# One of three dense tiles' gates put into a cleared DRAM table by GpSimd's adding scatters, and 52 low halves made by VectorE

## The reference, cut to what matters

```python
q = (xt @ wq).reshape(t_len, 8, 2, 64)
sub = jnp.einsum('thpd,hpkd->thpk', q, subkeys)        # 128 keys a half
s_top, i_top = lax.top_k(sub, 16)
cand = s_top[:, :, 0, :, None] + s_top[:, :, 1, None, :]
sc, ci = lax.top_k(cand.reshape(t_len, 8, 256), 16)
i1 = take(i_top[:, :, 0], ci // 16); i2 = take(i_top[:, :, 1], ci % 16)
eid = (i1 * 128 + i2).reshape(t_len, 128)              # 128 picks of 16384 experts a token
gate = jax.nn.softmax(sc, axis=-1).reshape(t_len, 128)
h = gelu(jnp.einsum('cd,ced->ce', xc, u[ec]))
out = jnp.einsum('ce,ced->cd', gate * h, v[ec])
```

## Time and profile before

| | before |
|---|---|
| median of 3 runs | 1693.93 us (1693.28 to 1694.68) |
| span of the profiled execution | 1695.2 us |
| TensorE busy | 1674.3 us (99%) |
| VectorE busy | 1206.4 us (71%) |
| GpSimd busy | 810.8 us (48%) |
| ScalarE busy | 779.4 us (46%) |
| moved by DMA | 417.63 MB, 246 GB/s on the mean |

### The profile page before, as it was taken

How to read it: one execution, slowest core, us unless ns; L and a number is a source line. 1 busy time by engine, 2 the same in 40 slices (tenths; PEclk the granted TensorE clock), 3 DMA queues, 4 the chain that set the end, 5 groups by cost and what they waited for, 6 DMA issues and landing times.

```text
span 1695.2 us, 24483 instructions
## 1 busy us (share of the span) xinstructions
PE 1674.3 (99%) x9013; PEld 1481.6 (87%) x9013; DVE 1206.4 (71%) x2480; ACT 779.4 (46%) x1318; POOL 810.8 (48%) x491
## 2 busy tenths in 40 slices
PE   9999999999999999999999999999999999999997
PEld 7778777788899999999999999999888888888886
DVE  3586895511164885989888988434988888888886
ACT  4545545522324345773675477433333333333332
POOL 5332233444542667776776776774433323323312
...
DMA  5121121242421566997899799997999999999952
GB/s 205 63 75 50 63 75 63 100 139 98 143 94 44 184 215 211 373 381 252 287 386 359 226 332 371 370 369 293 405 389 355 367 387 347 383 382 347 389 194 87
DMA packets 126502, 417.63 MB, mean 246 GB/s; under 512 B 12976, under 2 KB 32432, under 8 KB 124848
## 3 DMA queue, kind: packets, MB, share of 16 engines
...
q0 software_dynamic: 36864, 134.23, 21.1%
q10 hardware_dynamic: 19200, 49.03, 7.4%
...
...
## 4 chain that ended last, share of the span: by engine, by line
PE 90%; DMA 3%; DVE 3%; POOL 2%; ACT 1%; issue 1%; SPq 0%; ACTq 0%; DVEq 0%
PE ps L1364 17%; PE ps L1365 17%; PE ps L1366 17%; PE ps L1626 10%; PE ps L1624 10%; PE ps L1623 10%; PE ps L1734 5%; PE ps L1476 1%; DMA raw<-u_units 1%; PE ps L1428 1%; POOL w_lo L500 1%; POOL w_lo L458 1%; PE ps L1459 1%; DMA raw<-w_units 1%; DMA u_got<-u_rows,eid 1%
## 5 line engine op out<-in xcount | busy, mean ns | idle before, releaser
L557 ACT ACTIVATE w_hi<-raw 128x1024 fp32r<-128x1024 f32 x330 | 348.9, 1058 | 395.0 <-PE ps L1626 294.4
L1364 PE MATMUL ps<-tok_hi,w_hi 128*128 128x384 f32 (+1 forms) x1472 | 525.9, 357 | 3.1 <-ACT gelu_t L748 1.7
L1365 PE MATMUL ps<-tok_lo,w_hi 128*128 128x384 f32 (+1 forms) x1472 | 516.9, 351 | 0.0
L1366 PE MATMUL ps<-tok_hi,w_lo 128*128 128x384 f32 (+1 forms) x1472 | 516.9, 351 | 0.0
L500 POOL TENSOR_TENSOR w_lo<-raw,w_hi 128x1024 fp32r<-128x1024 f32 x128 | 318.4, 2490 | 166.1 <-ACT w_hi L557 165.0
L458 POOL TENSOR_TENSOR w_lo<-raw,w_hi 128x1024 fp32r<-128x1024 f32 x76 | 181.7, 2395 | 318.0 <-ACT w_hi L557 317.8
L1364 PEld LDWEIGHTS ps<-tok_hi,w_hi 128*128 128x128 f32 x1472 | 276.5, 188 | 33.8 <-issue 12.0
L1623 PE MATMUL ps<-w_hi,gh_hi 128*128 128x512 f32 x760 | 295.7, 389 | 0.0
L1624 PE MATMUL ps<-w_lo,gh_hi 128*128 128x512 f32 x760 | 295.7, 389 | 0.0
L517 POOL DMA_INDIRECT v_got<-v_rows,eid x128 | 150.0, 1172 | 304.1 <-DVE own L1148 286.9
L1366 PEld LDWEIGHTS ps<-tok_hi,w_lo 128*128 128x128 f32 x1472 | 276.3, 188 | 18.1
...
## 6 DMA issues: line engine op xcount, KB each, us to landing
raw<-u_units SPq DMA_DIRECT2D x128, 512.0 KB
raw<-v_rows SPq DMA_DIRECT2D x128, 512.0 KB
raw<-w_units SPq DMA_DIRECT2D x78, 512.0 KB
...
```

The lines of the kernel that those rows point to most:

```text
L557: act.activation(hi_of(n), raw[:, n % RAW, :], ACT.Copy).then_inc(hi_done, 1)
L1364: pe.matmul(out_, l_hi, r_hi, start=start, stop=False)
L1365: pe.matmul(out_, l_hi, r_lo, start=False, stop=False)
L1366: return pe.matmul(out_, l_lo, r_hi, start=False, stop=stop)
```

## The change

The gates of tile 1 no longer go through TensorE. SP clears the first four of the twelve bodies of `gate_d` with 16 stores of zeros of 512 KB (`clear_gates`, issued among the loads of units 8 to 23; the zeros are written by GpSimd once, in `zero`). VectorE works out for each token and pick the address in the table (`put_at`) and leaves the gates in `g_put`. GpSimd then issues 128 indirect DMAs, one a pick (`put_gate`), which add 4 bytes for each of the 128 tokens at their places in the table. Two heads of a token can pick the same expert, while the 16 picks of one head are all different: so every sixteenth put first waits until all earlier ones have landed.

Only 64 quads are left. Their two stages now have 26 units each, and a unit has one or two quads (`quads_in`). The units are laid out anew: routing of tile 1 in units 16 to 29, of tile 2 in 30 to 43, mark stage 2 in 44 to 69, routing of tile 3 in 70 to 83, mark stage 3 in 84 to 109, tail from 110. Two lists of points (`PACE`) set how many dots and puts must be out by which unit. VectorE makes the low halves of two in three units of the mark stages and of all in the tail (`low_on_dve`, `unit_lo`): 17 + 17 + 18 = 52 of 128 by the program's table; GpSimd keeps 76.

```diff
 
 DT = S - P
 NB = DT // TOK
-N_QUAD = DT // 4
-FIRST_UNITS, ROUTE_UNITS, MARK_UNITS = 16, 14, 16
-TAIL = FIRST_UNITS + 3 * (ROUTE_UNITS + MARK_UNITS)
-ROUTE_DOTS, MARK_DOTS = (3, 6, 6), 30
+PUT_TOK = P
+PUT_BODIES = PUT_TOK // TOK
+N_QUAD = (DT - PUT_TOK) // 4
+FIRST_UNITS, ROUTE_UNITS, MARK_UNITS = 16, 14, 26
+MARK_AT = {2: FIRST_UNITS + 2 * ROUTE_UNITS, 3: FIRST_UNITS + 3 * ROUTE_UNITS + MARK_UNITS}
+ROUTE_AT = {1: FIRST_UNITS, 2: FIRST_UNITS + ROUTE_UNITS, 3: MARK_AT[2] + MARK_UNITS}
+TAIL = MARK_AT[3] + MARK_UNITS
+PACE = {"dots": ((FIRST_UNITS + 6, 0), (ROUTE_AT[2], 3), (MARK_AT[2], 7), (ROUTE_AT[3], 45), (MARK_AT[3], 50),
+                 (TAIL, 90), (P - 4, P)),
+        "puts": ((ROUTE_AT[2] + 1, 0), (MARK_AT[2], 13), (ROUTE_AT[3], 59), (MARK_AT[3], 72), (TAIL, 118),
+                 (TAIL + 5, P))}
 U_SLOTS, V_SLOTS = 5, 6
 FMA_START, FMA_END = 2, P - 12
 KEPT = 8
 GATE_GROUP, GELU_GROUP = 16, 4
 
 
-def routed_at(j):
-
-    return FIRST_UNITS + (j - 1) * (ROUTE_UNITS + MARK_UNITS)
-
-
-def dots_before(b):
-
-    return sum(ROUTE_DOTS[:b]) + MARK_DOTS * b
+def by_unit(kind, k):
+
+    points = PACE[kind]
+    for (k0, n0), (k1, n1) in zip(points, points[1:]):
+        if k < k1:
+            return n0 + max(0, n1 - n0) * max(0, k + 1 - k0) // (k1 - k0)
+    return points[-1][1]
 
 
 def dots_by(k):
 
-    if k < FIRST_UNITS:
-        return 0
-    b, at = divmod(k - FIRST_UNITS, ROUTE_UNITS + MARK_UNITS)
-    if k >= TAIL:
-        return min(P, dots_before(3) + (P - dots_before(3)) * (k - TAIL + 1) // (P - TAIL - 4))
-    if at < ROUTE_UNITS:
-        return dots_before(b) + ROUTE_DOTS[b] * max(0, at - 6) // (ROUTE_UNITS - 7)
-    return dots_before(b) + ROUTE_DOTS[b] + MARK_DOTS * (at - ROUTE_UNITS + 1) // MARK_UNITS
+    return by_unit("dots", k)
+
+
+def quads_in(k):
+
+    return range(32 * k // MARK_UNITS, 32 * (k + 1) // MARK_UNITS)
+
+
+def low_on_dve(k):
+
+    return MARK_AT[2] <= k < ROUTE_AT[3] and k % 3 > 0 or MARK_AT[3] <= k < TAIL and k % 3 > 0 or TAIL <= k < P
+
+
+LOW_DVE = [k for k in range(P) if low_on_dve(k)]
+LOW_POOL = [k for k in range(P) if not low_on_dve(k)]
 
 
 def right_by(q):
...
                 sp.dma_start(gelu_in[m % 2][:], gelu_d[:, first:first + GELU_GROUP, :])\
                     .then_inc(gelu_back[m % 2], 16)
 
+            def clear_gates(i):
+
+                body, line = i // 4, P // 4 * (i % 4)
+                if i == 0:
+                    sp.wait_ge(zero_set, 1)
+                sp.dma_start(gate_d[body, :, line:line + P // 4, :].rearrange("p j t -> p (j t)"), zero[:])\
+                    .then_inc(zeros_out, 16)
+
             for j in range(P):
                 load_unit(U_EXP + j, u_units[j])
+                if 8 <= j < 8 + 4 * PUT_BODIES:
+                    clear_gates(j - 8)
                 if j == P - 8:
                     sp.wait_ge(gate_read, N_QUAD)
                     for s in range(2):
-                        sp.wait_ge(stage_out[s], 16 * (NB // 2))
+                        sp.wait_ge(stage_out[s], 16 * (NB - PUT_BODIES) // 2)
+                    sp.wait_ge(put_out, 16 * P)
                     load_gates(0, 0)
                 if j == P - 4:
                     load_gates(0, 1)
...
                 if e >= U_SLOTS:
                     pool.wait_ge(dot_done, e - U_SLOTS + 1)
                 elif e == 3:
-                    pool.wait_ge(pick_set, 2)
+                    pool.wait_ge(put_set, 1)
                 pool.indirect_dma_start(
                     out=u_got[e % U_SLOTS][:], out_offset=None, in_=u_rows,
                     in_offset=bass.IndirectOffsetOnAxis(ap=eid[:, e:e + 1], axis=0)).then_inc(u_in[e % U_SLOTS], 16)
...
                     out=v_got[e % V_SLOTS][:], out_offset=None, in_=v_rows.rearrange("p a d -> (p a) d"),
                     in_offset=bass.IndirectOffsetOnAxis(ap=eid[:, e:e + 1], axis=0)).then_inc(v_in[e % V_SLOTS], 16)
 
-            got = [0]
+            def put_gate(e):
+
+                if e == 0:
+                    pool.wait_ge(zeros_out, 16 * 4 * PUT_BODIES)
+                    pool.wait_ge(put_set, 1)
+                elif e % EK == 0:
+                    pool.wait_ge(put_out, 16 * e)
+                pool.indirect_dma_start(
+                    out=gate_d.rearrange("b p j (t o) -> (b p j t) o", o=1),
+                    out_offset=bass.IndirectOffsetOnAxis(ap=put_at[:, e:e + 1], axis=0),
+                    in_=g_put[:, e:e + 1], in_offset=None, compute_op=ALU.add).then_inc(put_out, 16)
+
+            got, put = [0], [0]
+
+            def puts_to(n):
+                while put[0] < min(n, P):
+                    put_gate(put[0])
+                    put[0] += 1
 
             def rows_to(n):
                 while got[0] < min(n, P):
...
                     got[0] += 1
 
             for k in range(FIRST_UNITS):
+                if k == 4:
+                    pool.wait_ge(sub_full, 16)
+                    pool.memset(zero[:], 0.0).then_inc(zero_set, 1)
                 expert_lo(k)
             pool.wait_ge(eid_set, 1)
             rows_to(3)
             for k in range(FIRST_UNITS, P):
-                expert_lo(k)
+                if not low_on_dve(k):
+                    expert_lo(k)
                 rows_to(dots_by(k - 1) + U_SLOTS if k >= FIRST_UNITS + ROUTE_UNITS else 3)
+                puts_to(by_unit("puts", k))
             rows_to(P)
             for s in range(2):
-                pool.wait_ge(stage_out[s], 16 * (NB // 2))
+                pool.wait_ge(stage_out[s], 16 * (NB - PUT_BODIES) // 2)
             for e in range(P):
                 get_v(e)
             pool.wait_ge(ln2_in, 32)
...
                 dve.tensor_tensor(w_lo[:, n % RAW, :], raw[:, n % RAW, :], w_hi[:, n % RAW, :].bitcast(F32),
                                   ALU.subtract).then_inc(lo_dve, 1)
 
+            def unit_lo(k):
+
+                n = U_EXP + k + LO_AHEAD
+                dve.wait_ge(hi_done, n + 1)
+                dve.tensor_tensor(w_lo[:, n % RAW, :], raw[:, n % RAW, :], w_hi[:, n % RAW, :].bitcast(F32),
+                                  ALU.subtract).then_inc(lo_dve, 1)
+
             def dot(e):
 
                 dve.wait_ge(u_in[e % U_SLOTS], 16 * (e // U_SLOTS + 1))
...
                 if b == 0:
                     dve.scalar_tensor_tensor(eid[:], pick[:, 0, :], float(NK), pick[:, 1, :], ALU.mult, ALU.add)\
                         .then_inc(eid_set, 1)
+                if b == 1:
+                    dve.wait_ge(lane_set, 1)
+                    settled(dve.tensor_scalar(part, lane, 5, None, ALU.logical_shift_right))
+                    dve.scalar_tensor_tensor(first_at, part, float(P * P * TOK - TOK), lane, ALU.mult, ALU.add)
+                    settled(dve.scalar_tensor_tensor(c_row[:], pick[:, 0, :], float(NK), pick[:, 1, :], ALU.mult, ALU.add))
+                    dve.tensor_scalar(put_at[:], c_row[:], float(TOK), first_at, ALU.mult, ALU.add)
                 dve.wait_ge(gexp_done, b + 1)
                 g = pick[:, 2, :].rearrange("p (h k) -> p h k", h=EH)
                 settled(dve.tensor_reduce(g_sum[:, 0, :], g, mybir.AxisListType.X, ALU.add))
                 settled(dve.reciprocal(g_sum[:, 1, :], g_sum[:, 0, :]))
-                to = g_own if b == 0 else pick[:, 2, :]
-                dve.tensor_tensor(to[:].rearrange("p (h k) -> p h k", h=EH), g,
+                to = (g_own[:], g_put[:], pick[:, 2, :], pick[:, 2, :])[b]
+                dve.tensor_tensor(to.rearrange("p (h k) -> p h k", h=EH), g,
                                   g_sum[:, 1, :].unsqueeze(2).to_broadcast([P, EH, EK]), ALU.mult)\
-                    .then_inc(pick_set, 1)
+                    .then_inc(put_set if b == 1 else pick_set, 1)
 
             def spread_picks(b):
 
-                dve.wait_ge(pickT_full, b)
-                if b > 1:
-                    dve.wait_ge(gate_full, 32 * (b - 1))
+                dve.wait_ge(pickT_full, b - 1)
+                if b == 3:
+                    dve.wait_ge(gate_full, 32)
                 dve.tensor_copy(g_T[:], ps[:, 5, 2 * P:3 * P]).then_inc(pickT_set, 1)
 
             def mark(q):
...
             route(0)
             dve.wait_ge(own_x, 1)
             for b in range(1, NT):
-                parts = iter([dots_before(b - 1) + ROUTE_DOTS[b - 1] * i // 3 for i in (1, 2, 3)])
+                parts = iter([dots_by(ROUTE_AT[b] + ROUTE_UNITS * i // 3 - 1) for i in (1, 2, 3)])
                 route(b, lambda: dots_to(next(parts)))
+                if b == 1:
+                    continue
                 spread_picks(b)
                 for k in range(MARK_UNITS):
-                    for quad in (2 * k, 2 * k + 1):
-                        mark(32 * (b - 1) + quad)
-                    dots_to(dots_by(routed_at(b) + ROUTE_UNITS + k))
+                    if low_on_dve(MARK_AT[b] + k):
+                        unit_lo(MARK_AT[b] + k)
+                    for quad in quads_in(k):
+                        mark(32 * (b - 2) + quad)
```

(12 more changed lines are left out.)

62 lines of the change are left out of this document (36 added, 26 removed).

## The result

| | before | changed |
|---|---|---|
| median of 4 runs each, same chip | 1693.72 us (1693.28 to 1694.68) | 1798.92 us (1796.56 to 1801.37) |
| ratio to before | | 1.0617, 95% interval 1.0602 to 1.0633 |
| span of the profiled execution | 1695.2 us | 1796.8 us |

The changed kernel is 105 us slower. I had forecast 1673.0, in a range of 1662 to 1708, and gave 0.24 to slower.

A forecast was written before the change was run, and what follows sets the result against it. TensorE was taken as the bound, the DMA engines as second limit. 1695.2 - 28.6 (quads) - 0.3 (transposes) + 4 (GpSimd's waits) + 4 (tail) = 1674.3 us profiled, 1673.0 median; range 1662 to 1708.

The forecast's parts named there:

- The bound and TensorE's loss: TensorE is the bound, busy 1674.3 of 1695.2 us; dropping 32 of 96 quads and three transposes saves 28.9 us.
- The clearing: Units 8 to 23: 16 stores of 512 KB, costed at nothing; 23 us of the DMA engines if uncovered.
- VectorE: Loses 49.0 us, gains 52 low halves at 1.24, 64.5 us; fits mark stages, and the tail if no dot waits.
- The put's price: GpSimd, units 44 to 110: put spacing 1.25 us, bounds 1.25 to 1.47; 313.5 us of work against TensorE's 331.8.
- rival C: GpSimd becomes the bound between units 44 and 110: 1705 us, or 1728 with spacing 1.47; chance 0.23.
- a put longer than 1.5 us: Sign on GpSimd that would by itself overturn the forecast, as would a landing over 8 us.
- What a put costs that is priced right: GpSimd, unit 44 to the tail: waits 10 us over the free 18, mostly hidden; 4 us left on the path.
- The waits for landings: On GpSimd every sixteenth put waits until earlier ones have landed: seven waits of 4 us, 28 us.
- The clock: TensorE's granted clock read 1.00 in every expert window shown, so it got no term.
- Rival D: Put packets cost the DMA engines as much as big ones, 155 ns: 1770 us, at half price 1705; chance 0.06.
- The tail: From unit 110: 33.9 MB in 74.9 us, 17 or 9 us too many, VectorE's lead covers 13; 4 left.
- Rival E: VectorE is the bound in the tail with no lead left, 17 us back in full: 1686 us; chance 0.07.

The follow-up runs named there:

- plain put: The changed kernel with puts that write instead of adding: 1739.31 us, ratio 1.0268.
- The writes without DMA: Kernel without puts, with later gathers and 24 dots in the tail, given six or four GpSimd scratch writes per put: 1804.03 and 1714.61 us.
- the evened order: The changed kernel with later routing gathers and 24 instead of 38 dots in the tail: 1671.82 us without puts, 1792.07 with adding puts.

## Why the prediction was wrong

**The bound and TensorE's loss: right.** 512 passes where 768 were, and mark stages of 136.2 and 135.3 us without the puts, for the 136.7 of the sum (its terms make 136.8). **The clearing: right.** It stands among the first 30 units, and they took 117.8 us with it and without it.

**VectorE: right alone, not beside the puts.** The low halves alone change the time by 0.15%. In the changed kernel, though, VectorE's 52 low halves took 82.8 us, not 64.5. Their median is 1.22 us, but the 16 that lasted longer than 1.3 us in the mark stages all ran while GpSimd made a low half of its own: the one at 767.67 lasted 4.01 us, beside GpSimd's from 767.65. Without the puts the longest is 1.27. What this is worth in time no run took apart.

**The put's price: the step that failed.** "It makes one descriptor per partition as the gather does, so I bound its spacing by the gather's 1.25 below and by the mean of the v gathers, 1.17 + 0.30 = 1.47, above, and take 1.25, since the u gathers are issued in the same stages." The median is 1.58 + 0.30 = 1.88, and 2.01 with everything that stands before it. For a plain put the step holds (0.99 + 0.30 = 1.29, between the bounds); what I had no row for was the adding, and I took the bounds as if it had none. With 2.01 and 1.35 in my own sum GpSimd has 401 us for TensorE's 331.8. That is rival C's mechanism and my own mark for it ("a put longer than 1.5 us"), but at a price past its worst case, 1728. Both bounds came from gathers, so the range could not hold the result.

**What a put costs that is priced right: the second step that failed.** "I leave 4 us on the path." Plain puts cost 45.0. By the rows of that kernel GpSimd's list for the three stages is 345 us, from 32 low halves at 2.49, 82 gathers at 1.33 and 105 puts at 1.49 with all that stands before them; that is 13 over TensorE's 331.8, and the stages took 366. So the list costs more than its excess. My sum took the three stages as one pool, while the loss stands in single stages (12.0 us in the routing stage between, 15.7 in the second mark stage), where by my reading the list, the gathers that wait for a slot and the waits for landings meet; no run takes these three apart.

**The waits for landings: wrong in size.** I took 7 waits of 4 us; six of the seven show, together 12.4, none over 3.2 (with plain puts 19.8, none over 6.6). The chain of the changed kernel has six landings of 4.1 to 6.1 us from the start of the issue; this is one:

```profile
751.70 5.83 DMA gate_d<-g_put,put_at
```

But the issue of this put itself takes 1.56 of that, and GpSimd issued a gather meanwhile, so only 3.22 was left to wait for. "DMA: Bandwidth & Descriptors" of the Trainium skill, in its anatomy of a DMA from GpSimd, gives some 2.0 us as the constant; the 5.83 is well over it, in a queue that holds gathers too. The Trainium skill's page "Perfetto Trace Analysis", under DMA Instruction — SWDGE (GPSIMD), says that such a record ends when the descriptors are made, not when the data has moved. This trace agrees: the put's record ends 1.56 us after its start, and its landing comes 5.83 us after it.

**The clock: put at nothing.** The prediction says that "the clock is no term here", from windows of a kernel without long holes. The changed kernel has 34.4 us more of TensorE's busy time for the same instructions than the kernel without puts and with even dots, at a granted clock of 0.87 to 0.97 in the stages with puts for 1.00. This is no cause of its own: where TensorE has no long holes the clock is 1.00, so it is part of what the holes cost.

**Rival D, packets: wrong.** The software queue's 18432 more packets raised its share of 16 engines from 21.1% of 1695.2 to 22.5% of 1796.8, by 46.6 us, which is 40 ns each, not 155; and the DMA share fell in the mark stages. The writes without DMA settle it: they cost as much.

**The routing stages: not in the sum at all.** I costed the change of stages and not the pace of the gathers in them. A gather in routing waits for a dot that VectorE makes only between the parts of its long routing work. Before, the gathers ran late enough (0.5 us of such waits; 39.4 after); now GpSimd stood 9.4 us before one, and the low halves behind it. With the puts in place this was 17 us. It hurts more where GpSimd is short of time: without the puts it waits longer for slots, 117.3 us in the expert part, and the routing stages lose 8.8 us in all.

**The tail: mis-sized.** "I leave 4 us on the path", from 17 or 9 us too many less 13 of lead. Without puts it was 23.2 over (98.1 for 74.9), with 14 dots fewer 5.6, at 393 GB/s. Rival E named this place, at 17 us. The bytes were too few: 398 GB/s over the 93 us of the window are 37.0 MB, not 33.9, since the stage also issues the first six gathers of `v` rows (3.1 MB), which my list lacks. Nothing of the excess was hidden: with 38 dots and with 24 the DMA engines stood at 1.02 and 1.00 and moved 398 and 393 GB/s, so I read the tail's length as that of its bytes. Why the lead of 13 us did not help is argued, not shown: the low halves that wait in the tail stand behind dots that wait for the same crowded engines.

In sum: 1665.0 for TensorE's work; 6.8 for what the evened order still loses; 22.5 for the pace of gathers and dots; 104.6 for the puts, 45.0 of it as plain puts and 59.6 for adding. That is 1798.9. The terms are differences between kernels in this order and depend on it: in the evened order the puts cost 120.3.
